# Second block's scores: high and low queries stacked, keys held twice, softmax ratios on GpSimd

## What is computed

```
h = rmsnorm(x, norm_g[l]);  proj = h @ w_in[l]                      # 1024 -> 4096
out_a = neighborhood_attention(q_a, k_a, v_a, rpb)                   # NA: 8 heads of 64, 8 x 16 window
out_b = diff_attention(q_b, k_b, v_b, t5_table, lam, ...)            # DA: 4 heads, two halves of 64
    logits = einsum('bqhtd,bkhtd->bhtqk', q, k) * scale              #   t = 0, 1
    p = softmax(logits + bias);  attn = p[:, :, 0] - lam * p[:, :, 1]
    out = rmsnorm(attn @ v, subln_g) * (1 - lam_init)
x = x + concat(out_a * silu(g_a), out_b * silu(g_b)) @ w_out[l]
```

## Time and profile before

| | us |
|---|---|
| median of 3 runs | 941.06 (940.94 to 941.32) |
| the profiled execution | 941.23 |
| its span, first to last instruction | 939.4 |
| mean granted clock of TensorE | 0.996 of full speed |

### The profile page before, as it was taken

One profiled execution on the slowest core, in us unless ns is written; L12 is line 12 of the kernel. 1 busy time (PEld: TensorE's weight loads), 2 busy tenths in 40 slices (PEclk: granted clock), 3 DMA queues, 4 the chain that ended last, 5 costly groups with the idle time before them and its releaser, 6 DMA issues.

```text
span 939.4 us, 14917 instructions
## 1 busy us (share of the span) xinstructions
PE 906.4 (96%) x5861; PEld 715.3 (76%) x5861; DVE 587.7 (63%) x1200; ACT 450.7 (48%) x962; POOL 70.3 (7%) x89
## 2 busy tenths in 40 slices
PE   3999999999999999999999999999999999999996
PEld 1689888865667788887888877888887788887785
DVE  5899798998886472438862448344255965335733
ACT  4734223666784243436925348233434863436631
POOL 1001130006300010000010000000000010000002
PEclk9999999999999999999999999999999999999999
DMA  9735636266000232332304224122243222333203
GB/s 380 312 109 125 181 136 180 102 209 239 1 2 23 90 129 90 112 101 76 111 8 150 90 90 134 43 90 90 90 155 92 62 91 89 94 100 118 72 0 90
DMA packets 34647, 104.71 MB, mean 111 GB/s; under 512 B 14929, under 2 KB 14929, under 8 KB 32146
## 3 DMA queue, kind: packets, MB, share of 16 engines
q1 hardware_dynamic: 28098, 85.77, 27.5%
q0 software_dynamic: 3824, 15.73, 5.2%
q10 hardware_dynamic: 2656, 2.26, 1.0%
HBM read 98.37 MB, written 4.19 MB: 109 GB/s over the span
## 4 chain that ended last, share of the span: by engine, by line
PE 88%; DVE 6%; ACT 2%; issue 2%; DMA 1%; SPq 0%; POOL 0%; POOLq 0%; DVEq 0%; ACTq 0%
PE bank L1023 81%; PE bank L1384 2%; PE bank L1522 2%; DMA ring<-in_w_ada 1%; PE bank L1364 1%; DVE ring L2083 1%; PE bank L1440 1%; DVE arena L1651 0%; DVE ring L2282 0%; ACT ring L834 0%; PE bank L1430 0%; ACT arena L715 0%; DVE soft L2115 0%; ACT w_hi L882 0%; DVE soft L2093 0%
## 5 line engine op out<-in xcount | busy, mean ns | idle before, releaser
L2138 DVE TENSOR_TENSOR w_lo<-ring,w_hi 128x1024 fp32r<-128x1024 f32 x80 | 97.8, 1225 | 114.6 <-ACT w_hi L882 111.5
L1023 PE MATMUL bank<-w_hi,hT_hi 128*128 128x512 f32 x320 | 125.3, 392 | 1.3 <-issue 1.0
L1023 PE MATMUL bank<-hT_hi,w_hi 128*128 128x512 f32 x320 | 126.3, 395 | 0.0
L1023 PE MATMUL bank<-hT_lo,w_hi 128*128 128x512 f32 x320 | 124.6, 389 | 0.0
L1023 PE MATMUL bank<-hT_hi,w_lo 128*128 128x512 f32 x320 | 124.6, 389 | 0.0
L1023 PE MATMUL bank<-w_lo,hT_hi 128*128 128x512 f32 x320 | 124.6, 389 | 0.0
L1023 PE MATMUL bank<-w_hi,hT_lo 128*128 128x512 f32 x320 | 124.5, 389 | 0.0
L882 ACT ACTIVATE w_hi<-ring 128x1024 fp32r<-128x1024 f32 x80 | 84.4, 1058 | 11.6 <-PE bank L1023 11.4
L1023 PEld LDWEIGHTS bank<-w_hi,hT_hi 128*128 128x128 f32 x320 | 60.1, 188 | 14.7 <-issue 2.6
L1023 PEld LDWEIGHTS bank<-hT_hi,w_hi 128*128 128x128 f32 x320 | 60.1, 188 | 14.0 <-issue 0.7
L1023 PEld LDWEIGHTS bank<-hT_lo,w_hi 128*128 128x128 f32 x320 | 60.1, 188 | 12.8
(11 more groups left out here) (323 smaller groups left out, 1814.1 us busy)
## 6 DMA issues: line engine op xcount, KB each, us to landing
ring<-in_w_units SPq DMA_DIRECT2D x80, 512.0 KB, 3.6
ring<-in_w_ada SPq DMA_DIRECT2D x4, 2048.0 KB, 10.2
bias_ring<-in_na_bias POOLq DMA_DIRECT2D x8, 1024.0 KB, 5.5
ring<-in_w_out SPq DMA_DIRECT2D x2, 2048.0 KB, 8.7
bias_ring<-in_t_bias POOLq DMA_DIRECT2D x8, 448.0 KB, 3.8
x_t<-in_x SPq DMA_DIRECT2D x4, 512.0 KB, 5.9
arena<-in_w_ada SPq DMA_DIRECT2D x1, 2048.0 KB, 20.3
arena<-in_w_ada SPq DMA_DIRECT2D x2, 1024.0 KB, 23.2
```

Of the source, the lines that this page charges most:

```text
L1023: return pe.matmul(out, lhsT, rhs, start=first, stop=last)
L2138: dve.tensor_tensor(w_lo[:, u % 4], raw_w[:, u % 4], w_hi[:, u % 4].bitcast(fp32), SUB).then_inc(S["w_split"], 1)
```

## The change

Instead of q_hi, q_lo, k_hi and k_lo there are q_a, q_b, k_a, k_b and k_lo. q_a[t] holds the first half's high part on partitions 0 to 63 and the same half's low part on 64 to 127; q_b[t] the second half's low part on 0 to 63 and its high part on 64 to 127. k_a[t] holds the first half's high keys twice, above each other, k_b[t] those of the second half. High x high and low x high are then one product of 128 rows for each half; high x low stays one of 64 rows. ScalarE and VectorE write each q and k tile by two instructions of 64 partitions. GpSimd copies the keys to the other partitions (`keys_twice`), and makes the reciprocals and ratios (`ratio`) that VectorE made in `combine`. k_b's tiles lie partly over other tensors (the gains, the tail of the rows), so the DMA of the gains now waits for the last take of the NA loop. Three semaphores that were used once are merged away; a constant of -1 is set at the start.

```diff
@@ GpSimd
+            def keys_twice(l, half, t):
+
+                pool.wait_ge(S["qk_hi"], 16 * l + 8 * half + 4 + t + 1)
+                settle(pool.tensor_copy(k_a[HD:P, t, :], k_a[0:HD, t, :]))
+                pool.tensor_copy(k_b[t][0:HD, :], k_b[t][HD:P, :]).then_inc(S["k_twice"], 1)
+                pool.wait_ge(S["k_twice"], 8 * l + 4 * half + t + 1)
+
+            def ratio(l, j):
+
+                k = 2 * (N_DA * l + j)
+                pool.wait_ge(S["exp_done"], k + 2)
+                r0, r1_ = (slice((k + t) % 8, (k + t) % 8 + 1) for t in range(2))
+                inv = rinv[:, k % 16:k % 16 + 2]
+                pool.tensor_tensor(rg[:, r1_], ssum[:, r0], lam[:, l:l + 1], MUL)
+                settle(pool.tensor_tensor(inv, ssum[:, k % 8:k % 8 + 2], minus_1, ALU.pow))
+                pool.tensor_tensor(rg[:, r1_], rg[:, r1_], inv[:, 1:2], MUL).then_inc(S["rg_ready"], 1)
...
                 if l:
-                    pool.wait_ge(S["xn_ready"], NT * (l + 1))
+                    pool.wait_ge(S["na_taken"], 2 * N_NA * l)
                 pool.dma_start(gain, io["gains"][l]).then_inc(S["gain_in"], 16)
                 x_rstd(l)
...
                 at_ = LOADS * l
-                for n in range(at_ + (2 if l else 0), at_ + DAH + 2):
-                    load_bias(n)
+                if l == 0:
+                    load_bias(0)
+                    load_bias(1)
+                for t in range(4):
+                    keys_twice(l, 0, t)
+                    for j in EARLY.get(t - 1, ()):
+                        ratio(l, j)
+                for j in range(N_EARLY, N_DA):
+                    ratio(l, j)
+                    if j % NT == NT - 1:
+                        load_bias(at_ + 2 + j // NT)
                 pool.wait_ge(S["o_stats"], l + 1)
                 inv_root(DAV, SUB_EPS, "o_rstd", lambda v: v[:, 0:NT * DAH])
+                for t in range(4):
+                    keys_twice(l, 1, t)
@@ ScalarE
                 if kind in ("qa", "qb"):
-                    act.activation(q_hi[:, t, :], src[:, :], ACT.Copy, scale=SCALE).then_inc(S["qk_hi"], 1)
+                    act.activation(q_a[0:HD, t, :], src[0:HD, :], ACT.Copy, scale=SCALE)
+                    act.activation(q_b[HD:P, t, :], src[HD:P, :], ACT.Copy, scale=SCALE).then_inc(S["qk_hi"], 1)
                 elif kind in ("ka", "kb"):
-                    act.activation(k_hi[:, t, :], src[:, :], ACT.Copy).then_inc(S["qk_hi"], 1)
+                    act.activation(k_a[0:HD, t, :], src[0:HD, :], ACT.Copy)
+                    act.activation(k_b[t][HD:P, :], src[HD:P, :], ACT.Copy).then_inc(S["qk_hi"], 1)
@@ TensorE, na_score
+                pe.wait_ge(S["k_twice"], 8 * l + 4 + p + 1)
...
-                for n, (q_, k_) in enumerate(((q_hi, k_hi), (q_lo, k_hi), (q_hi, k_lo))):
-                    for e in range(2):
-                        hf = slice(e * HD, (e + 1) * HD)
-                        ins = mm(bank[S_BANKS[(2 * m + e) % 4]][:, 0:KW], q_[hf, p, toks], k_[hf, p, keys], n == 0, n == 2)
...
+                outs = [bank[S_BANKS[(2 * m + e) % 4]][:, 0:KW] for e in range(2)]
+                for e, (q_, k_) in enumerate(((q_a, k_a[:, p]), (q_b, k_b[p]))):
+                    mm(outs[e], q_[:, p, toks], k_[:, keys], True, False)
+                for e, q_ in enumerate((q_a, q_b)):
+                    hf = slice(e * HD, (e + 1) * HD)
+                    mm(outs[e], q_[hf, p, toks], k_lo[hf, p, keys], False, True).then_inc(S["na_scored"], 1)
@@ TensorE, score_2: now a unit j, both halves, of the same form with 512 keys
+                        pe.wait_ge(S["k_twice"], 8 * l + h + 1)
@@ VectorE, combine
-                        dve.wait_ge(S["exp_done"], k + 2)
-                        r0, r1_ = (slice((k + t) % 8, (k + t) % 8 + 1) for t in range(2))
-                        dve.reciprocal(rinv_0[:, j % 8:j % 8 + 1], ssum[:, r0])
-                        settle(dve.reciprocal(rinv[:, r1_], ssum[:, r1_]))
-                        stt(rg[:, r1_], ssum[:, r0], lam[:, l:l + 1], rinv[:, r1_], MUL, MUL)
+                        dve.wait_ge(S["rg_ready"], u0 + j + 1)
+                        r1_ = slice((k + 1) % 8, (k + 1) % 8 + 1)
@@ VectorE, low parts
-                                dve.scalar_tensor_tensor(lo_[:, t, :], bank[(pt2(l, g) + t) % 4][:, :], SCALE if isq else 1.0,
-                                                         hi_[:, t, :].bitcast(fp32), MUL, SUB).then_inc(S["proj_evac"], 1)
+                                out_a, out_b = (q_a[HD:P, t, :], q_b[0:HD, t, :]) if isq else (k_lo[0:HD, t, :], k_lo[HD:P, t, :])
+                                hi_a, hi_b = (q_a[0:HD, t, :], q_b[HD:P, t, :]) if isq else (k_a[0:HD, t, :], k_b[t][HD:P, :])
+                                src = bank[(pt2(l, g) + t) % 4]
+                                dve.scalar_tensor_tensor(out_a, src[0:HD, :], SCALE if isq else 1.0, hi_a.bitcast(fp32), MUL, SUB)
+                                dve.scalar_tensor_tensor(out_b, src[HD:P, :], SCALE if isq else 1.0, hi_b.bitcast(fp32), MUL, SUB)\
+                                    .then_inc(S["proj_evac"], 1)
```

More of the change, by code:

```diff
@@ L94, in build @@
             x_hi = cut(low.enter_context(nc.sbuf_tensor("x_hi", [P, KD * T], fp32r))[:, :], k=KD, t=T)
+            low.enter_context(nc.sbuf_tensor("xn_rows_gap", [P, 2 * NG * (T + 2 * CS) + N_ROWS - T], fp32r))
+            k_b_rows = low.enter_context(nc.sbuf_tensor("k_b_rows", [P, T], fp32r))[:, :]
+            low.enter_context(nc.sbuf_tensor("cons_soft_gap", [P, -(-N_CONS // 8) * 8 + 4 * T], fp32r))
+            k_b_gain = low.enter_context(nc.sbuf_tensor("k_b_gain", [P, 2 * T], fp32r))[:, :]
         ring = sb("ring", SLOTS * SLOT)
@@ L128, in build @@
         second = ctx.enter_context(ExitStack())
-        q_hi, q_lo, k_hi, k_lo = (cut(sb2(n, 4 * T, fp32r)[:, :], h=4, t=T) for n in ("q_hi", "q_lo", "k_hi", "k_lo"))
+        q_a, q_b, k_a, k_lo = (cut(sb2(n, 4 * T, fp32r)[:, :], h=4, t=T) for n in ("q_a", "q_b", "k_a", "k_lo"))
         bias_ring = cut(sb2("bias_ring", 4 * 1024)[:, :], b=2, j=2048)
@@ L135, in build @@
         w_hi, w_lo = (cut(sb2(n, 4 * UNIT, fp32r)[:, :], u=4, n=UNIT) for n in ("w_hi", "w_lo"))
+        k_b0 = sb2("k_b0", T, fp32r)[:, :]
         prob2 = cut(ring[:, 0:SLOT], b=8, t=T)
@@ L141, in build @@
         gain = soft[:, 4 * T:6 * T]
+        k_b = [k_b0, k_b_gain[:, 0:T], k_b_gain[:, T:2 * T], k_b_rows]
         v_mid = cut(xn_t[:, 0:(NT - 1) * 512], i=NT - 1, f=512)
@@ L239, in build @@
         rg = stat(8)
-        rinv_0 = stat(8)
+        minus_1 = stat(2)
         lam = stat(LAYERS)
@@ L512, in _ @@
             settle(pool.memset(mhalf, -0.5))
+            settle(pool.memset(minus_1, -1.0))
             settle(pool.memset(gate_b[:, :], 0.0))
@@ L1350, in _ @@
                 ins.then_inc(S["cp_T"], 1)
-            def score(k, products, width):
-                if k >= 4:
-                    pe.wait_ge(S["scores_taken"], k - 3)
-                for m, (lhsT, rhs) in enumerate(products):
-                    ins = mm(bank[S_BANKS[k % 4]][:, 0:width], lhsT, rhs, m == 0, m == len(products) - 1)
-                ins.then_inc(S["scores_done"], 1)
             def turn(u, src, blocks, ready, count):
@@ L1553, in _, with score_2 @@
                         pe.wait_ge(S["o_used"], u0 + N_DA)
-                    def score_2(e):
-                        i, h = UNITS_DA[e // 2]
-                        q_at = (slice(e % 2 * HD, (e % 2 + 1) * HD), h, slice(i * P, (i + 1) * P))
-                        k_at = (q_at[0], h, slice(0, T))
-                        score(k0 + e, [(q_hi[q_at], k_hi[k_at]), (q_lo[q_at], k_hi[k_at]), (q_hi[q_at], k_lo[k_at])], T)
+                    def score_2(j):
+                        i, h = UNITS_DA[j]
+                        toks = slice(i * P, (i + 1) * P)
+                        pe.wait_ge(S["k_twice"], 8 * l + h + 1)
+                        outs = [bank[S_BANKS[(k0 + 2 * j + e) % 4]][:, :] for e in range(2)]
+                        for e, (q_, k_) in enumerate(((q_a, k_a[:, h]), (q_b, k_b[h]))):
+                            if k0 + 2 * j + e >= 4:
+                                pe.wait_ge(S["scores_taken"], k0 + 2 * j + e - 3)
+                            mm(outs[e], q_[:, h, toks], k_, True, False)
+                        for e, q_ in enumerate((q_a, q_b)):
+                            hf = slice(e * HD, (e + 1) * HD)
+                            mm(outs[e], q_[hf, h, toks], k_lo[hf, h, :], False, True).then_inc(S["scores_done"], 1)
                     for g in range(4 - 4 * half, 8 - 4 * half):
@@ L1586, in _ @@
                                     if half:
-                                        score_2(2 * m)
-                                        score_2(2 * m + 1)
+                                        score_2(m)
                                     else:
@@ L1594, in _ @@
                             if j < N_DA:
-                                score_2(2 * j)
```

(7 more changed lines are left out.)

12 lines of the change are left out of this document (4 added, 8 removed).

## The result

The changed kernel takes 968.9 us (median of 4, 967.91 to 970.89) against 941.1 (940.94 to 941.32): a ratio of 1.030, 95% interval 1.028 to 1.032. It is 27.8 us slower, and 968 was forecast.

A forecast was written before the change was run, and what follows sets the result against it. TensorE, busy 906.4 of 939.4 us, was taken as the bound. 941.2 + 18.2 (DA-head stall) + 2.0 (clock) + 2.3 (halves) + 0.8 + 4.8 (NA division changes) - 1.0 (tail) = 968.3, forecast 968 us, range 956 to 978.

The forecast's parts named there:

- The term that decides: DA loop's head: early combines wait for GpSimd ratios queued behind key copies that need tile evacuations; 18.2 us.
- The walk: Step-by-step timing of layer 1's DA head, tile 2's evacuation to take(3), which came out 9.1 us late; chance 0.57.
- The 18.2 us: Stall at the DA loop's head: take(3) 9.1 us late in each of two layers, nothing caught up after.
- The gain in columns is zero: Score products: three old pairs fill 3 slots, two full products and one pair also 3, so no TensorE time saved.
- The extra division change in NA: NA rounds: full product to pair costs one more array division change, 0.20 us, 24 rounds, 4.8 us.
- The double scores ahead of the NA loop: Two units scored in a row before the NA loop: 0.40 us a layer, 0.8 us in all.
- The same 0.40 us a layer at units 1 and 2: DA head, two units scored in a row after tile 2: one exit and one entry of the array division more, 0.40 us.
- The strict order: DA scores: products strictly in issue order, saving 14.5 us, sum 953.8; rejected; as a rival with the stall, 962, chance 0.03.
- The NA head: Start of the NA loop: evacuating the last k tile in halves delays TensorE 1.15 us a layer, 2.3 in all.
- The clock: Low-clock stretches at both DA heads: 1.5 us a layer, less 1.0 already in layer 0, +2.0 us; bounds 0 and 5.
- The tail's credit: DA loop's tail: VectorE relieved of the ratios gains 0.5 us a layer, -1.0 us in the sum.

The follow-up runs named there:

- the first two runs: Changed kernel with GpSimd's early ratios ahead of the keys' copies, 958.96 us; changed kernel with reciprocals and ratios back on VectorE, 957.68 us.
- the fourth run: Changed kernel with the DA scores as three pairs of 64 rows again, copies still made: 968.98 us.
- the first run: Changed kernel with GpSimd's ratios of the early units ahead of the copies of the tile behind which they stood: 958.96 us.
- the second run: Changed kernel with reciprocals and ratios back on VectorE, GpSimd only copying the keys: 957.68 us.

## Why the prediction was right

**The term that decides.** The walk said: combine(0) 725.87, take(1) 728.99, end of the low part 739.82, take(3) 740.97. The trace, less 15.86: 725.73, 729.07, 739.68, 740.91. So take(3) is 9.02 us later than before, 9.1 forecast, and 9.03 in layer 0 (444.00 against 434.27, with the layer's start 0.70 later). TensorE's second transposes are 8.2 us late where 8.4 was forecast: 6.83 is the recorded wait, and the other 1.4 is time lost before it, 0.4 of it waiting for take(1). The walk met the time although every price in it was a little off: two copies stepped at 1.37 us (1.60 forecast), a ratio took 1.14 (1.25), and what they saved went back into the halves of the last tile: ScalarE's two 1.26 us (748.62 to the copy at 749.88) against 1.10, VectorE's two 1.42 (754.10 to 755.52) against 1.30. The right part was the order in which the engines take their programs; the reordered kernel shows it is worth 10 us alone. The 0.50 and 0.65 us by which one half follows the other are too short: the trace has 0.61 and 0.69 (748.62 to 749.23, 754.10 to 754.79), since the overlap with the next instruction of the earlier trace rows is not there between the halves.

The 18.2 us are not all of that order, though. They hold the halves, which the runs price at 8.1 us in all, 2.4 of it NA's. The prediction had them in the walk as four steps (1.10, 1.30, 1.10 and 1.30 again), without saying what the halves would cost had the ratios been early. My numbers for the first two runs fell over that. When one part of a chain of waits is undone, the next one takes its place, and a term of a sum can't simply be struck out.

**The products.** "The gain in columns is zero" held: DA rounds stay at 2.38 us, and the fourth run shows nothing. The extra division change in NA was taken from the 0.09 + 0.11 us at a pair's entry and measured 0.20; twelve rounds 2.39 us (2.4 forecast). The double scores ahead of the NA loop cost 0.38 and 0.39 us (0.40). That changing the division drains the array is what the Trainium skill, TensorEngine Tiling (Array Packing), Key Properties, states. The NA runs agree in that each further change costs time, 0.20 us. The same 0.40 us a layer at units 1 and 2 was named and left out of the sum, rightly here, since take(3) sets the time. From tile 2's last matmul to tile 3's it is 7.68 us with the full products and 7.26 with DA's old scores, 0.42 more in both layers. Where the stall is gone it should show in the whole time: the medians of the two runs with the copies and NA's old scores differ by 1.2 us, 0.8 expected, but in the traces of these two the clock's stretches hide it.

**The strict order.** The trace's pairs were taken against the rule of the Trainium skill, TensorE: Matmul & The Clock Gate, Part 3, that matmuls start and end in program order. The run with alternating halves bears the trace out, against that rule: products of different row halves run beside each other when the code has three of one before three of the other. By the rule the time would have been 953.8; 968.9 was measured.

**The NA head.** 2.3 us forecast, 2 x 1.18 measured. TensorE's wait for the last low part was 0.28 us and is 1.58 in layer 0, as the same view of the changed kernel shows:

```profile
574.08 0.66 PE L1552 MATMUL bank<-cons,ring 128*128 128x128 f32 x4 [1.58 <-DVE k_lo L2341]
```

**The clock.** This is the term that was mis-sized, in place and in size. Forecast were stretches at both DA heads, 1.5 us each. In layer 1 the DA part grew by 9.85 us, 9.02 of them up to take(3); the rest, 0.83, is the clock less the 0.62 us that the tail and head gain from VectorE's relief, so about 1.45. But the stretch at the NA head of layer 0, behind the wait of 1.58 us, was not foreseen: 36.66 against 33.71 is 2.95 us in the profiled execution, and the median is 2 us lower than that execution. That one costs more though it is shorter: TensorE is busy for all of its 6.8 us, while the first 3.1 of the 10.2 us in layer 1 fall in the long wait, and behind the slow transposes TensorE waits 0.96 us for take(3) anyway. The tail's credit of 0.5 us a layer measured 0.62. The prediction also read a cause into the earlier trace rows that the trace does not have: ahead of that stretch TensorE waits 0.53 and 0.55 us, at 435.02 and 437.14, not about 2.

Against the median the sum is 0.6 us low, against the profiled execution 2.6. The errors that cancel: DA 1.1 less than forecast, the first block 0.7 and the NA head's clock 3.0 more. In the trace of the run with DA's old scores, which took 969.14 us, the DA parts are 19.8 us longer than before (19.2 forecast) and the NA parts 7.1 (7.1 forecast). So the sums of the two parts are right to about a us there, and the rest is mostly the clock, which differs from trace to trace; that the median lies within 0.6 us of the sum is in part luck.

## What to carry to other kernels

Work moved to an idle engine is paid for by its place in that engine's program: here the same ratios cost about 1 us ahead of the copies (within the scatter) and 11 behind them, because the copies wait for an engine that waits for the ratios. Price an instruction by the length of a partition: splitting a 128-partition evacuation into two halves doubled it, and in the end cost 8 us here, with nothing gained for it. And before merging matrix products, look whether the small ones already run beside each other; the merged form gave nothing here, and a further change of the array's division cost 0.20 us each time.

## What was not expected of the hardware

- A copy from one half of the partitions to the other on GpSimd, 64x512, takes 0.61 us against 0.71 for 128x512 on the same partitions; I had allowed up to 1.4. It is cheap, and its place is dear. A copy that stays on its partitions was not run at this size.
- VectorE's combine takes 0.75 us alone, and took 1.18 us at 740.54 of the first run, starting 0.03 us before a GpSimd copy, and again at the same place in layer 0. In these heads four copies took 0.79 to 1.05 us instead of 0.61. A low part, with one input in PSUM, started at 738.00 of the second run beside two copies and took its usual 0.68 us, and the copies theirs. So an idle GpSimd isn't free for VectorE. What the two share was not tried.
- A wait of 1.58 us of TensorE stands at all 18 NA heads of the nine traces with the halves. In four of them it is followed by a stretch at half the clock: 6.8 us in layer 0 of the changed kernel and in layer 1 of the second run (ratios back on VectorE), 3.4 in layer 0 of the first run and of the one with copies and NA's old scores. In the other fourteen by none, in the changed kernel's own layer 1 (887.44) among them. What tips it is open.
